# Pool's input projection by seven block products each for columns and gates, with the trailing means under the second

## The reference, cut to what matters

```python
def trailing_mean(u, window):
    cs = jnp.cumsum(u.astype(jnp.float32), axis=1)
    lagged = jnp.pad(cs, ((0, 0), (window, 0), (0, 0)))[:, :seq]
    count = jnp.minimum(jnp.arange(1, seq + 1), window)
    return (cs - lagged) / count[None, :, None]

def pool_mixer(h, in_w, group_w, group_b, scale, out_w):
    u, gate = jnp.split(h @ in_w, 2, axis=-1)
    ug = u.reshape(b, s, 4, 256)
    pooled = jnp.stack([trailing_mean(ug[:, :, g], w) for g, w in enumerate((2, 4, 8, 16))], axis=2) - ug
    mixed = jnp.einsum('bsgc,gcd->bsgd', pooled, group_w) + group_b
    y = mixed.reshape(b, s, 1024) * scale * jax.nn.silu(gate)
    return y @ out_w
```

## Time and profile before

| what | value |
|---|---|
| time, median of 3 runs | 1745.78 us (1745.27 to 1746.69) |
| the profiled execution | 1745.65 us, its span 1743.9 us |
| PE busy | 1718.4 us, 99% of the span |
| DVE busy | 1163.4 us, 67% |
| ACT busy | 710.2 us, 41% |
| POOL busy | 243.4 us, 14% |
| DMA | 280.66 MB, mean 161 GB/s |

### The profile page before, as it was taken

One profiled execution on the slowest core, in us unless ns is written; L12 is line 12 of the kernel. 1 busy time (PEld: TensorE's weight loads), 2 busy tenths in 40 slices (PEclk: granted clock), 3 DMA queues, 4 the chain that ended last, 5 costly groups with the idle time before them and its releaser, 6 DMA issues.

```text
span 1743.9 us, 20943 instructions
## 1 busy us (share of the span) xinstructions
PE 1718.4 (99%) x8377; PEld 1448.1 (83%) x8377; DVE 1163.4 (67%) x1466; ACT 710.2 (41%) x1082; POOL 243.4 (14%) x238
## 2 busy tenths in 40 slices
PE   7999999999999999999999999999999999999998
PEld 7888887888998888888888888888888888888886
DVE  5653565544997866589848866984887357444497
ACT  4332466653996331543233323323344245222133
POOL 2000011201774215100000000000002133000101
PEclk9999999999999999999999999999999999999999
DMA  5678977797653781283182256227211113122032
GB/s 183 243 267 320 331 259 248 238 335 193 143 134 123 239 291 60 104 301 128 64 296 92 90 202 232 83 77 284 99 49 49 49 61 115 56 84 73 1 144 97
DMA packets 137745, 280.66 MB, mean 161 GB/s; under 512 B 9456, under 2 KB 29488, under 8 KB 134192
## 3 DMA queue, kind: packets, MB, share of 16 engines
q1 hardware_dynamic: 137648, 279.33, 47.0%
HBM read 212.16 MB, written 67.14 MB: 160 GB/s over the span
## 4 chain that ended last, share of the span: by engine, by line
PE 91%; DVE 5%; ACT 1%; DMA 1%; issue 1%; SPq 0%; POOLq 0%; POOL 0%; ACTq 0%; DVEq 0%
PE PS L747 13%; PE PS L748 13%; PE PS L749 13%; PE PS L994 11%; PE PS L996 11%; PE PS L995 11%; PE PS L723 4%; PE PS L886 2%; PE PS L887 2%; PE PS L888 2%; PE PS L908 2%; PE PS L1098 1%; PE PS L1097 1%; PE PS L1096 1%; PE PS L928 1%
## 5 line engine op out<-in xcount | busy, mean ns | idle before, releaser
L1106 ACT ACTIVATE WH<-WB 128x2048 fp32r<-128x2048 f32 x56 | 107.3, 1917 | 286.2 <-PE PS L996 239.2
L747 PE MATMUL PS<-UH,RHL 128*128 128x512 f32 (+1 forms) x512 | 191.0, 373 | 2.4 <-DVE UL L1551 2.1
L1551 DVE TENSOR_TENSOR WB<-WB,WH 128x2048 fp32r<-128x2048 f32 x56 | 128.2, 2289 | 97.3 <-ACT WH L1106 97.3
L749 PE MATMUL PS<-UH,RHL 128*128 128x512 f32 (+1 forms) x512 | 189.7, 370 | 0.0
L748 PE MATMUL PS<-UL,RHL 128*128 128x512 f32 (+1 forms) x512 | 189.6, 370 | 0.0
L994 PE MATMUL PS<-WH,AH 128*128 128x512 f32 x448 | 174.8, 390 | 1.0 <-DVE H L1915 0.6
L994 PE MATMUL PS<-AH,WH 128*128 128x512 f32 x448 | 174.6, 390 | 0.0
L996 PE MATMUL PS<-WH,AL 128*128 128x512 f32 x448 | 174.3, 389 | 0.0
L996 PE MATMUL PS<-AH,WB 128*128 128x512 f32 x448 | 174.3, 389 | 0.0
L995 PE MATMUL PS<-WB,AH 128*128 128x512 f32 x448 | 174.3, 389 | 0.0
L995 PE MATMUL PS<-AL,WH 128*128 128x512 f32 x448 | 174.3, 389 | 0.0
(11 more groups left out here) (268 smaller groups left out, 3813.5 us busy)
## 6 DMA issues: line engine op xcount, KB each, us to landing
WB<-in_w_ff SPq DMA_DIRECT2D x32, 1024.0 KB, 9.3
AH<-uf_scratch SPq DMA_DIRECT2D x21, 1024.0 KB, 5.3
AL<-uf_scratch SPq DMA_DIRECT2D x21, 1024.0 KB, 7.5
GX<-gates_scratch SPq DMA_DIRECT2D x64, 256.0 KB, 3.7
gates_scratch<-GST SPq DMA_DIRECT2D x56, 256.0 KB, 4.4
H<-in_x SPq DMA_DIRECT2D x16, 512.0 KB, 8.7
RAW<-in_w_in SPq DMA_DIRECT2D x16, 512.0 KB, 7.3
UH<-ugT_scratch SPq DMA_DIRECT2D x8, 1024.0 KB, 8.3
```

The source lines that it names most:

```text
L747: pe.matmul(o_ap, sh, mh, start=first, stop=False)
L749: ins = pe.matmul(o_ap, sl, mh, start=False, stop=last)
L1106: return act.activation(dst, src, ACT.Copy, **more)
L1551: return dve.tensor_tensor(dst, src, high.bitcast(F32), ALU.subtract)
```

## The change

Columns and gates each become one unit of seven block products, as the feed-forward has them: unit 0 makes u^T into UA (SBUF), unit 1 the gates into UF. PE now reads a weight block as the wide operand and one of seven token forms (u's blocks and four sums, `pool_tok_sum`). The forms are split in unit 0, stored to DRAM (`pool_form`) and loaded again for unit 1 (`pool_form_again`). The results are copied by ACT (`pool_copy`) or added by DVE (`pool_add`) into SBUF. The trailing means read and write UA under unit 1, with all their shifts on GpSimd; the group products stand inside steps 9 to 12; the gates are SiLU'd and scaled block by block (`gate_open`, `gate`), then multiplied in (`gated_means`). The way out takes its seven products in another order, and shares WH with the unit before. The ring is no longer used here. The diff, cut (a line of "..." where lines are left out):

```diff
-        S_pi = [(slab256(w_pi, 0, 256 * g), slab256(w_pi, 0, D + 256 * g), slab256(w_gr, 256 * g, 0, 2)) for g in range(4)]
...
+        pool_kinds = [Kind(1, 0, True), Kind(2, 4, True), Kind(5, 4, True), Kind(6, 0, False), Kind(7, 0, False), Kind(3, 4, False),
+                      Kind(4, 0, True)]
+        pool_kinds += [Kind(1, 0, True), Kind(2, 4, True), Kind(6, 0, False), Kind(7, 0, False), Kind(5, 4, True),
+                       Kind(3, 4, False), Kind(4, 0, True)]
...
+        i_copies = {0: (0, 0), 2: (1, 1), 3: (0, 1), 4: (1, 0), 7: (0, 0), 9: (0, 1), 10: (1, 0)}
+        i_adds = (1, 4, 5, 6, 8, 11, 12, 13)
...
+        po_kinds = [Kind(1, 4, True), Kind(4, 0, True), Kind(6, 4, False), Kind(7, 4, False), Kind(2, 0, True), Kind(5, 0, True),
+                    Kind(3, 0, False)]
...
-            for g in range(4):
-                su, sg, sw = S_pi[g]
...
+            def pool_step(n, between=None):
+                kind, a = pool_kinds[n], act_slot(n)
+                for s in range(4):
+                    b, q = kind.bank + s, slice(P * s, P * s + P)
+                    take(b, *i_freed(n, s))
+                    on.wait_ge(*pi_wl.of(n))
+                    on.wait_ge(*(pi_tl.of(n) if n < 7 else pf_in[a].of(n, 1)))
+                    for k in range(4):
+                        sh, sl, mh, ml = WH[n % 2][:, k, q], i_wide_lo(n, k, q), AH[a][:, k, :], AL[a][:, k, :]
+                        pe.matmul(bank(b), sh, mh, start=(k == 0 and kind.fresh), stop=False, skip_group_check=True)
+                        pe.matmul(bank(b), sh, ml, start=False, stop=False, skip_group_check=True)
+                        ins = pe.matmul(bank(b), sl, mh, start=False, stop=(k == 3), skip_group_check=True)
+                    ins.then_inc(*pi_sum.up(n, s))
+                    if between and s in between:
+                        between[s]()
+            to_u("pool", 5)
+            pool_step(0, {0: lambda: to_u("pool", 6), 2: lambda: to_u("pool", 7)})
+            for n in range(1, 14):
...
+            def pool_wide_high(n):
+                u, name = n // 7, g_wide[pool_kinds[n].p]
+                on.wait_ge(*(pi_in[name].of(u) if name[0] == "A" else pi_wsum.of(u, name)))
+                if n == 0:
+                    on.wait_ge(*p_turned.of(1, 1))
+                elif n == 1:
+                    on.wait_ge(*pp_sum.of(1, 7))
+                else:
+                    on.wait_ge(*pi_sum.of(n - 2, 3))
+                copy(WH[n % 2], i_wide(n)).then_inc(*pi_wh.up(n))
...
             for t in ts:
                 opened(t, 1, 2 * (t % 2))
+                if t == 5:
+                    pool_wide_high(0)
                 if t == 7:
-                    split_to(S_pi[0][0].idx[1])
+                    pool_tok_high(0)
                 if t >= 3:
-                    u_hi("pool", t - 3)
+                    u_copy(t - 3, "pool")
                 sum_h("final", t, pl_added_end.of(t))
                 if t:
...
+            pool_wide_high(1)
+            u_copy(5, "pool")
+            pool_tok_high(1)
+            u_copy(6, "pool")
+            u_copy(7, "pool")
+            pool_copy(0, 0)
+            pool_copy(0, 1)
+            pool_copy(0, 2)
+            group_high(0)
+            for n in range(1, 14):
+                if n - 1 in i_copies:
+                    pool_copy(n - 1, 3)
+                if n == 1:
+                    pool_tok_high(2)
+                if n < 13:
+                    pool_wide_high(n + 1)
+                if 2 <= n < 6:
+                    pool_tok_high(n + 1)
+                if n == 9:
+                    gate_open(0, 0)
+                if n == 12:
+                    gate_open(1, 1)
+                for i in {6: (0, 1), 7: (2,), 8: (3,), 9: (4,), 10: (6,)}.get(n, ()):
+                    mean_copy(*tiles[i])
+                if n == 8:
+                    mean_high(0, 0)
+                    mean_high(0, 1)
+                if n in i_copies:
+                    pool_copy(n, 0)
+                    pool_copy(n, 1)
+                if 9 <= n < 13:
+                    group_copy(n - 9)
+                if 9 <= n < 12:
+                    group_high(n - 8)
+                    if n == 11:
+                        mean_copy(*tiles[7])
+                    mean_high(n - 8, 0)
+                    if n == 9:
+                        mean_copy(*tiles[5])
+                    mean_high(n - 8, 1)
+                if n in i_copies:
+                    pool_copy(n, 2)
...
+                if t == 6:
+                    pool_wide_low(0)
                 if t == 7:
-                    split_to(S_pi[0][0].idx[1])
-                if t >= 3:
-                    u_lo("pool", t - 3)
+                    pool_tok_low(0)
                 if t:
                     in_place(t - 1)
                 if t >= 2:
                     norm("pool", t - 2, GB2)
             in_place(7)
+            pool_wide_low(1)
             norm("pool", 6, GB2)
-            def pooled(g, j):
-                b, w = 4 * (g % 2) + 2 * j, 2 << g
-                u = PS[:, b:b + 2, :].rearrange("p b c -> p (b c)")
-                ready = po_copied.of(g, j)
-                for n in range(g + 1):
-                    src, dst, s = WN[n % 2], WN[(n + 1) % 2], 1 << n
-                    if s in (1, 4):
-                        on.wait_ge(*ready)
-                        dve.tensor_tensor(dst[:, 16:1040], src[:, 16:1040], src[:, 16 - s:1040 - s], ALU.add).then_inc(
-                            *shift_dve.up(g, j, s))
-                    ready = (shift_dve if s in (1, 4) else shift_pool).of(g, j, s)
-                src, dst = WN[(g + 1) % 2], WN[g % 2]
-                on.wait_ge(*ready)
-                dve.scalar_tensor_tensor(out=dst[:, 32:1040], in0=src[:, 32:1040], scalar=1.0 / w, in1=u[:, 16:1024], op0=ALU.mult,
-                                         op1=ALU.subtract).then_inc(*po_main.up(g, j))
+            pool_tok_low(1)
+            norm("pool", 7, GB2)
...
+            def mean_main(i):
+                (g, j), r = tiles[i], i
+                u, src = UA[:, r, :], WN[(g + 1) % 2]
+                on.wait_ge(*shifted.of(g, j, g))
+                dve.scalar_tensor_tensor(out=u[:, 16:1024], in0=src[:, 32:1040], scalar=1.0 / (2 << g), in1=u[:, 16:1024],
+                                         op0=ALU.mult, op1=ALU.subtract).then_inc(*po_main.up(g, j))
...
+            def gate(i, h):
+                c = halved(UF, i, h)
+                on.wait_ge(*s_opened.of(i, h))
+                for s in range(4):
+                    r = 4 * i + s
+                    ins = dve.scalar_tensor_tensor(out=c[:, s, :], in0=c[:, s, :], scalar=psc[:, r:r + 1], in1=SB[i, h][:, s, :],
+                                                   op0=ALU.mult, op1=ALU.mult)
+                ins.then_inc(*z_done.up(i, h))
+            def gated_means(i, h):
+                c, y = halved(UF, i, h), halved(UA, i, h)
+                on.wait_ge(*z_done.of(i, h))
+                on.wait_ge(*m_copied.of(2 * i + 1, 1, 1))
+                for s in range(4):
+                    r = 4 * i + s
+                    ins = dve.scalar_tensor_tensor(out=y[:, s, :], in0=y[:, s, :], scalar=pgb[:, r:r + 1], in1=c[:, s, :],
+                                                   op0=ALU.add, op1=ALU.mult)
+                ins.then_inc(*y_done.up(i, h))
...
+            pool_tok_sum("T1")
+            pool_wide_sum(0, "S1")
+            pool_tok_low(2)
+            pool_wide_sum(0, "S2")
+            pool_wide_low(2)
+            pool_adds(1)
+            pool_tok_sum("T2")
+            pool_wide_sum(0, "S4")
+            pool_wide_low(3)
+            pool_tok_low(3)
+            pool_tok_sum("T4")
+            pool_tok_sum("T3")
+            pool_wide_sum(0, "S3")
+            pool_tok_low(4)
+            pool_wide_low(4)
+            pool_tok_low(5)
+            pool_wide_low(5)
+            on.wait_ge(*turned.of("pool", 7, 1))
+            for n in range(2):
+                dve.memset(WN[n][:, 0:16], 0.0).then_inc(*pads_set.up(n))
+            pool_adds(4, 0, 1)
+            pool_tok_low(6)
+            pool_adds(4, 2, 3)
+            pool_wide_low(6)
+            pool_adds(5, 0)
+            pool_wide_sum(1, "S1")
+            pool_adds(5, 1)
+            mean_main(0)
+            pool_adds(5, 2, 3)
+            pool_wide_sum(1, "S2")
+            pool_wide_sum(1, "S3")
+            pool_adds(6, 0)
+            mean_main(1)
+            pool_wide_low(7)
+            pool_adds(6, 1, 2, 3)
+            pool_wide_sum(1, "S4")
+            mean_main(2)
+            pool_wide_low(8)
+            group_low(0)
+            pool_wide_low(9)
+            mean_main(3)
+            mean_low(0)
+            pool_adds(8, 0, 1)
+            mean_low(1)
+            pool_adds(8, 2, 3)
+            pool_wide_low(10)
+            mean_main(4)
+            gate(0, 0)
+            group_low(1)
+            mean_low(2)
+            mean_main(5)
+            mean_low(3)
```

(149 more changed lines are left out.)

493 lines of the change are left out of this document (268 added, 225 removed).

## The result

The changed kernel takes 1769.16 us (median of 4, 1768.42 to 1771.03), the kernel before 1745.78: 1.0137 of it, with a 95% interval of 1.0124 to 1.0150. It is 23.4 us slower, where 1768.4 was forecast. PE's busy time fell by 10.4 us only (1718.4 to 1708.0), though 22.4 us of work were taken away: the rest came back as slow matmuls, and PE's waits come on top.

A forecast was written before the change was run, and what follows sets the result against it. PE was taken to bound the kernel, with 91% of the chain. From 1745.65 us, 22.4 spared, plus 42.1 of waits on ordered queues and 3 for the clock, gave 1768.4 us, range 1760 to 1773.

The forecast's parts named there:

- PE spared: Columns and gates: 672 matmuls in place of 768, some of those halves, saving PE 22.4 us.
- ahead of step 0: Before the first product, PE waits for token 5's norm and transposes on DVE: 5.6 us.
- step 7: Start of the second unit: PE waits for a DVE chain of 18.3 us against 10.9 of step 6: 7.4 us.
- group products 1, 2, 3: Inside steps 9 to 12, PE waits for copies, shifts, means and splits: 2.8, 2.3 and 6.9 us.
- product 1: Way out: DVE has 24.4 us of queued work against PE's 21.8, so PE waits 2.8 us.
- product 3: Way out: DVE's queue and H2's reload take 28.4 us against 22.5, so PE waits 5.9 us.
- banks: Small waits of PE at a bank: 0.3 us among the group products, 0.7 in the way out.
- clock: PE's granted clock falls at some waits over 3 us, 1.2 us lost each: 3 us taken, 7 at most.
- The rival priced at 7 to 14: The clock falls at each of PE's waits and stays down longer than at the start: 1772 to 1780 us, chance 0.20.
- The lock: GpSimd's shifts and DVE's two-input SBUF instructions exclude each other for whole instructions; 8 us of holds reach PE.
- no-lock rival: GpSimd and DVE share ports plainly, giving 34 us of waits: 1757 us (1747 to 1760), chance 0.19.
- Slack rival: PE's waits fall inside slack, below 22.4 us, so the kernel gets faster: 1723 to 1741 us, chance 0.12.

The follow-up runs named there:

- experiment 7: Changed kernel with the seven token-block forms neither stored nor read back, so steps 7 to 13 multiply stale blocks; 1770.08 us against 1769.16.
- Experiments 3 and 8: Two runs against the changed kernel: norm 6 and PE's transposes reordered around step 0, 1766.28 us; DVE's instructions in the way out reordered, 1764.09 us.
- order_gpsimd: Changed kernel with the same instructions in another order throughout, shifts staying on GpSimd; 1748.53 us.
- experiment 6: Changed kernel with all shifts on DVE and PE's four long waits filled with unread matmuls; 1757.15 us, 9.2 below the same without fills.
- experiment 10: Against the kernel reordered throughout with shifts on DVE (1739.03 us), a few more ACT and DVE instructions moved; 1733.10 us, 0.9927 of the kernel before.

## Why the prediction was right, point by point

| step | predicted | profile after |
|---|---|---|
| PE spared | 22.4 | account closes with 22.4 |
| ahead of step 0 | 5.6 | 5.30 |
| inside step 0 | 4.1 | 1.91 |
| step 4 | 3.3 | 3.11 |
| step 7 | 7.4 | 7.22 |
| group products 1, 2, 3 | 2.8, 2.3, 6.9 | 2.49, 1.80, 6.50 |
| product 1 | 2.8 | 2.67 |
| product 3 | 5.9 | 3.89 |
| banks | 1.0 | 0 |
| sum of waits | 42.1 | 34.9 |
| clock | 3 | 10.9 |
| forms' DMA | 0 | 0 (experiment 7) |

- **Places and sizes of the waits.** Each is where the sum had it, seven of nine within 0.5 us. Experiments 3 and 8 and order_gpsimd moved instructions only, to 20.6 us less in the last, so the ordered queues are shown to be their cause.
- **Slips in the sums.** Three of the listed sums don't come out: product 1 is 24.4 against 21.8, 2.6 and not 2.8; step 7's terms add up to 18.2, so 7.3; and the terms listed between groups 2 and 3 add up to 17.0 and not 18.0, 6.1 against 10.9 and not 6.9. Measured were 2.67, 7.22 and 6.50. By its own terms the sum of waits was 41.0.
- **Clock: the mis-sized term.** I took 3 us, bounded at 7 from the earlier trace rows; it was 10.9 (some 0.5 of it are single late starts behind waits at a clock of 1.00). The step that failed is the price of one fall: 1.2 us, from the start of the kernel, where PE ran 2.7 us at the low clock. That it was read from matmuls of 256 columns matters little, for there too somewhat under half of that time was lost. What was too small is the time: behind step 7 matmuls started 0.43 apart for 6.0 us (1559.04 to 1565.09), which lost 2.9, and behind group 3's wait for 4.0, which lost 1.9; ahead of and in step 0 2.2 were lost, behind products 1 and 3 1.6 and 1.7. I also took more than half of my bound of 7 to be absorbed; of the 10.9 it was a third. The rival priced at 7 to 14 was right on this term, though the clock didn't fall at each wait; its total would have been too high.
- **Why the total still fits.** The waits were 7.2 us shorter than predicted and the clock 7.9 dearer. The two are linked at two places only. The transposes of token 5 and the first starts of step 0 lost 0.9 + 1.3 us, and the wait behind them came out 2.2 shorter than walked; product 1's slow starts lost 1.6, and product 3's wait came out 2.0 shorter, 1.6 of them for that reason. There DVE was the late one anyway, and 3.8 us were given back. In the other stretches the clock's loss adds up in full (experiment 6). Of the 7.9 that leaves 4.1, and on the other side 3.4 of waits that I had too long (1.0 at banks, 2.4 in small parts): that these two met is luck.
- **The lock.** The holds are there: the four shifts of a tile of group 3 took 12.30 us beside DVE's work, those of the last tile 8.34 with the gated means away, and this sum of DVE ahead of step 7 took 3.98 where it takes 2.29 with the shifts on DVE:

```profile
1550.72 3.98 DVE L2267 TENSOR_TENSOR IW<-IWW,IW 128x2048 f32<-128x2048 f32 x1
...
1610.82 12.30 POOL L2637 TENSOR_TENSOR WN<-WN 128x1024 f32<-128x1024 f32 x4 [2.70 <-ACT WN L1151]
```

 At step 7 the sum had a hold of 1.8, the row shows 1.7, and the wait fits. But that all holds together cost PE 8 us here isn't shown: no run takes the lock away and leaves the shifts' length. The sum of waits, 34.9, even lies nearer to the 34 of the no-lock rival, which with a clock term of 10.9 would have given 1768 too. What speaks for the holds is the 3.8 given back at two waits, which makes 38.7, and the rows place by place. How much of the 8 reached the end stays open.
- **Slack rival.** It needed waits below 22.4 us. They are not, in this order; experiment 10 is that case, with 7.3, at 1733.
- The wait for H2's reload that I gave product 3 was DVE's add into H (L2493), as forecast.

## What to carry to other kernels

When the bounding engine is spared work, write down for each of its waits what the feeding engine has queued from the event that starts the chain to the instruction that ends it; the totals of busy time (DVE 69%) say nothing of it, and another order of the same instructions was worth 20.6 us here, with the shifts on DVE and one step more 36.1. Price each wait of the bounding engine with the clock it costs behind it: somewhat under half of the time that it then works at the low clock, 1.6 to 2.9 us here wherever it fell. And ask of each such loss whether the next wait takes it back: it does where the feeding engine's chain doesn't start from the late matmuls. A chain of short instructions can be better off on the busier engine: the shifts on DVE (69% busy) in place of GpSimd (16%) were worth 2.8 us in the old order and 9.5 in the tight one.
